# Dealing the query and key projections out beside the HGRN units, and moving twenty adaLN slabs beside the neighbourhood attention tiles

## The reference

```python
h = modulate(rms_norm(x, norm1_g[l]), sh1, sc1)          # latent and context
q, k, v, hq, hf, hb, hi, hg, ga, gh = split(h @ w_in[l])  # 12 blocks of 512 columns
o_na = neighbourhood_attention(rope(q), rope(k), v, ...)  # 8 heads, window + context keys
o_hg = hgrn2_bidirectional(silu(hq), hi, hf, hb)          # 4 heads, scans both ways
x = x + g1 * ((sigmoid(ga) * (o_na @ w_na_o) + sigmoid(gh) * (norm(o_hg) * silu(hg) @ w_hg_o)) @ w_out[l])
h2 = modulate(rms_norm(x, norm2_g[l]), sh2, sc2)
x = x + g2 * grouped_moe(h2)                              # 16 experts, top 2
```

## Time and profile before

| | us |
|---|---|
| median of 3 runs | 2262.05 (2261.82 to 2262.33) |
| the profiled execution | 2260.14 |
| its span, first to last instruction | 2258.3 |
| mean granted TensorE clock | 0.944 |
| HGRN loop, layer 0 / layer 1 (164.8 to 343.9 / 1397.7 to 1531.3) | 179.1 / 133.6 |
| attention tiles, layer 0 / layer 1 (425.6 to 509.0 / 1587.0 to 1639.0) | 83.4 / 52.0 |

### The profile page before, as it was taken

How to read it: one execution, slowest core, us unless ns; L and a number is a source line. 1 busy time by engine, 2 the same in 40 slices (tenths; PEclk the granted TensorE clock), 3 DMA queues, 4 the chain that set the end, 5 groups by cost and what they waited for, 6 DMA issues and landing times.

```text
span 2258.3 us, 21335 instructions
## 1 busy us (share of the span) xinstructions
PE 1986.0 (88%) x7884; PEld 1304.1 (58%) x7884; DVE 1134.5 (50%) x1562; ACT 777.5 (34%) x892; POOL 753.8 (33%) x276
## 2 busy tenths in 40 slices
PE   6998789989999789898999799789899788888886
PEld 2445555444444477777777454546388566666664
DVE  3146652473011566667665433532721576666664
ACT  2222221241000365455555122221410455555553
POOL 0004432100000175556665001423000356666663
PEclk8999999899999899999999799999899899999998
DMA  9330407201204165566554443315124266666661
GB/s 363 127 119 19 149 29 233 111 1 38 75 0 149 38 224 197 211 223 223 210 203 145 150 149 112 118 56 163 37 78 180 98 229 235 223 223 223 220 211 36
DMA packets 160809, 329.02 MB, mean 146 GB/s; under 512 B 21072, under 2 KB 22224, under 8 KB 160720
## 3 DMA queue, kind: packets, MB, share of 16 engines
q1 hardware_dynamic: 143312, 323.66, 39.9%
q10 hardware_dynamic: 17408, 4.20, 1.2%
HBM read 326.79 MB, written 1.05 MB: 145 GB/s over the span
## 4 chain that ended last, share of the span: by engine, by line
PE 58%; DVE 15%; POOL 11%; issue 10%; ACT 5%; DMA 1%; SPq 1%; PEldq 0%; DVEq 0%; POOLq 0%; ACTq 0%
PE bank L374 19%; POOL ring_lo L1220 11%; PE bank L385 5%; PE bank L589 4%; PE bank L577 4%; PE bank L646 3%; ACT w_hi L1087 2%; PE bank L751 2%; PE bank L720 2%; PE bank L444 2%; PE bank L341 2%; DVE ring_lo L1626 2%; DVE pick L1605 2%; DVE pickw L1609 2%; PE bank L549 2%
## 5 line engine op out<-in xcount | busy, mean ns | idle before, releaser
L1220 POOL TENSOR_TENSOR ring_lo<-ring,w_hi 128x2048 fp32r<-128x2048 f32 (+1 forms) x96 | 586.2, 6118 | 894.1 <-ACT w_hi L1087 894.1
L374 PE MATMUL bank<-hT,ring 128*128 128x512 f32 (+1 forms) x1280 | 479.8, 530 | 12.5 <-DVE hT L1307 12.0
L374 PEld LDWEIGHTS bank<-hT,ring 128*128 128x128 f32 x1280 | 246.7, 195 | 226.4 <-issue 198.6
L1087 ACT ACTIVATE w_hi<-ring 128x4096 fp32r<-128x4096 f32 x96 | 347.7, 3621 | 14.3 <-PEq L294 14.3
L1626 DVE TENSOR_TENSOR ring_lo<-ring,w_hi 128x2048 fp32r<-128x2048 f32 (+1 forms) x96 | 236.1, 2460 | 125.0 <-ACT w_hi L1087 124.8
L720 PE MATMUL bank<-ring_lo,picked_hi 128*128 128x512 f32 x512 | 141.6, 421 | 54.5 <-POOL ring_lo L1220 31.9
L1315 DVE SCALAR_TENSOR_TENSOR xT<-bank,mod,xT 128x256 f32<-128x256 f32 x216 | 97.6, 481 | 153.0 <-PE bank L751 77.4
L1177 POOL TENSOR_TENSOR dec<-pf 128x512 f32<-128x512 f32 (+1 forms) x32 | 28.2, 880 | 432.3 <-DVE pb L1352 288.1
L720 PEld LDWEIGHTS bank<-ring_lo,picked_hi 128*128 128x128 f32 x512 | 96.6, 197 | 94.0 <-POOL ring_lo L1220 46.5
L646 PE MATMUL bank<-hrow_hi,pick 128*128 128x512 f32 x192 | 95.2, 496 | 52.4 <-DVE pickw L1609 52.4
L715 PE MATMUL bank<-w_hi,picked_lo 128*128 128x512 f32 x512 | 128.4, 393 | 1.4 <-DVE picked_lo L1617 1.4
(11 more groups left out here) (207 smaller groups left out, 2912.2 us busy)
## 6 DMA issues: line engine op xcount, KB each, us to landing
ring<-in_w_gate SPq DMA_DIRECT2D x32, 2048.0 KB, 8.4
ring<-in_w_up SPq DMA_DIRECT2D x32, 2048.0 KB, 9.0
ring<-in_w_down SPq DMA_DIRECT2D x32, 2048.0 KB, 7.7
ring<-in_w_ada SPq DMA_DIRECT2D x24, 2048.0 KB, 13.8
ring<-in_w_in SPq DMA_DIRECT2D x24, 2048.0 KB, 8.4
ring<-in_w_out SPq DMA_DIRECT2D x4, 2048.0 KB, 10.5
bias_skew<-in_rel_bias_reversed ACTq DMA_DIRECT2D x64, 64.0 KB, 3.8
ring<-in_w_na_o SPq DMA_DIRECT2D x2, 2048.0 KB, 12.3
```

The source lines that it names most:

```text
L374: mm = T.matmul(o[:, lo:TOK], w[:, k, c * P:(c + 1) * P], hT[:, k, lo:TOK], start=(k == 0), stop=(k == KT - 1))
L1087: S.activation(w_hi[m % 2][:], ring[:, s, :], ACT.Copy).then_inc(sem["w_hi_ready"], 1)
L1220: G.tensor_tensor(ring_lo[:, s, a], ring[:, s, a], w_hi[(3 * e + g) % 2][:, a].bitcast(f32), ALU.subtract).then_inc(sem["w_lo_ready"], 1)
```

## The change

1. *Slabs.* The twenty later adaLN slabs leave the projections, the HGRN loop and the value, rope and gate stage. Slabs 4 to 19 are worked beside the attention tiles of layer 0, one at the end of every odd tile (1 to 31), slabs 20 to 23 in layer 1 at the ends of tiles 3, 6, 9 and 12 (`beside_tile`). The rows of slab m are followed by the turn of slab m-1; ScalarE copies in its tile n, VectorE adds in its iteration n + 4.
2. *Projections.* The 64 products of the query and key projections are dealt out over the 38 units, one or two behind each (`project_beside`). They have two PSUM banks (6 and 7) and a semaphore of their own; the loop's other work turns over six banks. ScalarE copies a finished projection two units later in its own order (`keep_beside`).
3. *Ring.* A list `lane` names the slot of each slab; a slab waits for the last one in its slot. The input slabs 3, 4, 5, 6, 0, 1, 2, 7 come first, then the adaLN slabs, then those of the merge. The experts' slabs keep n % 4.

```diff
-        loads = []
+        loads, lane = [], []
+        order = (2, 0, 3, 1)
...
 
         ada_loads = [("ada", l, s) for l in range(DEPTH) for s in range(12)]
...
+        lane += order
         for l in range(DEPTH):
-            a = ada_loads[12 * l + 4:12 * l + 16]
-            loads += [("in", l, 3), a[0], ("in", l, 4), a[1], ("in", l, 5), a[2], ("in", l, 6)]
-            loads += [("in", l, 0)] + a[3:6] + [("in", l, 1)] + a[6:9]
-            loads += [("in", l, 2)] + a[9:11] + [("in", l, 7)] + a[11:12]
+            loads += [("in", l, s) for s in (3, 4, 5, 6, 0, 1, 2, 7)]
+            turn = [0, 1, 2, 3, 0, 1, 2, 3]
+            loads += ada_loads[4:20] if l == 0 else ada_loads[20:24]
+            turn += [0, 1, 2, 3, 0, 1, 2, 3, 0, 1, 2, 3, 0, 1, 3, 1] if l == 0 else [0, 1, 3, 1]
             loads += [("in", l, 8), ("nao", l), ("in", l, 9), ("hgo", l), ("in", l, 10), ("in", l, 11)]
+            turn += [2, 3, 0, 1, 2, 3]
             loads += [("out", l, 0), ("out", l, 1)]
-            assert len(loads) % SLOTS == 0
+            turn += [0, 2]
+            lane += [order[x] for x in turn]
...
             for ph, n in ((2 * l, N_EXPERTS), (2 * l + 1, 3 * N_EXPERTS if l == 0 else N_EXPERTS)):
                 loads += [("moe", ph, e, k) for e in range(n) for k in range(3)]
+            lane += [n % SLOTS for n in range(len(lane), len(loads))]
...
-            return ring[:, slot_of(key) % SLOTS, :]
+            return ring[:, lane[slot_of(key)], :]
...
-            return slot_full[n % SLOTS], 16 * (n // SLOTS + 1)
+            return slot_full[lane[n]], 16 * lane[:n + 1].count(lane[n])
+
+        def last_in(n):
+
+            return max(m for m in range(n) if lane[m] == lane[n])
 
...
+        turns = [0]
+        main_banks = [8]
+        sides = [0]
...
+        def beside_tile(l, n):
+
+            if l == 0:
+                return 4 + n // 2 if n % 2 == 1 and 0 < n < 32 else None
+            return 19 + n // 3 if n in (3, 6, 9, 12) else None
...
-            def open_bank(key, who):
-
-                b = jobs[0] % 8
-                jobs[0] += 1
+            def open_bank(key, who, side=False):
+
+                if side:
+                    b = 6 + sides[0] % 2
+                    sides[0] += 1
+                    ready[key] = (b, sides[0], "side_ready")
+                else:
+                    b = turns[0] % main_banks[0]
+                    turns[0] += 1
+                    jobs[0] += 1
+                    ready[key] = (b, jobs[0], "psum_ready")
...
-                ada = 12 * l + 4
                 for s, who in ((3, "q_ready"), (4, "k_sig"), (5, "k_sig")):
                     pe.wait_ge(*full(("in", l, s)))
                     for c in range(4):
                         project(l, s, c, who, lo if s == 3 else 0)
-                        if c == 0 and s > 3:
-                            ada_turn(ada + s - 4)
-                    ada_rows(ada + s - 3)
                 pe.wait_ge(*full(("in", l, 6)))
                 for t in range(4):
                     project_rows(l, 6, t, "v_ready")
-                    if t == 0:
-                        ada_turn(ada + 2)
...
-                extra = [(s, c) for s in (0, 1) for c in range(4)]
-
-                def between():
-                    if not extra:
-                        return
-                    s, c = extra.pop(0)
-                    if c == 0:
-                        pe.wait_ge(*full(("in", l, s)))
-                    project(l, s, c, "naqk_ready", lo if s == 0 else 0)
-
+                main_banks[0] = 6
+                turns[0] = 0
+
+                def project_beside(first, end):
+
+                    for m in range(first, end):
+                        s, c, k = m // 32, m // 8 % 4, m % 8
+                        w = slot(("in", l, s)).rearrange("p (k n) -> p k n", k=KT)
+                        a = lo if s == 0 else 0
+                        if m % 32 == 0:
+                            pe.wait_ge(*full(("in", l, s)))
+                        if k == 0:
+                            beside[0] = open_bank(("in", l, s, c), "naqk_ready", side=True)
+                        mm = T.matmul(beside[0][:, a:TOK], w[:, k, c * P:(c + 1) * P], hT[:, k, a:TOK],
+                                      start=(k == 0), stop=(k == KT - 1))
+                        if k == KT - 1:
+                            mm.then_inc(sem["side_ready"], 1)
+                        if m % 32 == 31:
+                            slot_spent[slot_of(("in", l, s))] = (sem["side_ready"], sides[0])
+
+                beside = [None]
                 u = 38 * l
                 for hp in range(2):
                     for unit in range(19):
...
                         u += 1
-
-                        n = ada + 3 + 3 * hp + (unit - 5) // 4
-                        if unit in (5, 9, 13) and n < len(ada_loads):
-                            ada_rows(n)
-                        if unit in (7, 11, 15) and n < len(ada_loads):
-                            ada_turn(n)
-                        if unit % 4 == 3:
-                            between()
-                while extra:
-                    between()
+                        v = 19 * hp + unit
+                        project_beside(v * 64 // 38, (v + 1) * 64 // 38)
+                main_banks[0] = 8
 
...
-                if l == 0:
-                    ada_rows(13)
...
                         .then_inc(sem["psum_ready"], 1)
-                if l == 0:
-                    ada_turn(13)
...
                     project(l, 7, c, "hgate_ready", lo)
-                    if l == 0 and c == 0:
-                        ada_turn(14)
-                if l == 0:
-                    ada_rows(15)
                 pe.wait_ge(sem["rope_done"], 8 * (l + 1))
-                if l == 0:
...
+                    m = beside_tile(l, n)
+                    if m is not None:
+                        ada_rows(m)
+                        if m not in (4, 20):
+                            ada_turn(m - 1)
+                ada_turn((19, 23)[l])
...
-                    if n - SLOTS not in slot_spent:
+                    if last_in(n) not in slot_spent:
                         break
-                    sp.wait_ge(*slot_spent[n - SLOTS])
+                    sp.wait_ge(*slot_spent[last_in(n)])
...
-                        n = ada + 3 + 3 * hp + (unit - 6) // 4
-                        if unit in (6, 10, 14) and n < len(ada_loads):
-                            ada_keep(n)
-                        if unit % 4 == 0 and unit and extra:
-                            between()
+                        v = 19 * hp + unit - 2
+                        if v >= 0 and (v + 1) * 64 // 38 // 8 > v * 64 // 38 // 8:
+                            keep_beside()
...
+                    m = beside_tile(l, n)
+                    if m is not None:
+                        ada_keep(m)
...
+                    if m is not None:
+                        ada_mod(m)
                 if stop <= 10 * l + 4:
```

More of the change, by code:

```diff
@@ L209, in build @@
         loads += ada_loads[0:4]
+        lane += order
         for l in range(DEPTH):
-            a = ada_loads[12 * l + 4:12 * l + 16]
-            loads += [("in", l, 3), a[0], ("in", l, 4), a[1], ("in", l, 5), a[2], ("in", l, 6)]
-            loads += [("in", l, 0)] + a[3:6] + [("in", l, 1)] + a[6:9]
-            loads += [("in", l, 2)] + a[9:11] + [("in", l, 7)] + a[11:12]
+            loads += [("in", l, s) for s in (3, 4, 5, 6, 0, 1, 2, 7)]
+            turn = [0, 1, 2, 3, 0, 1, 2, 3]
+            loads += ada_loads[4:20] if l == 0 else ada_loads[20:24]
+            turn += [0, 1, 2, 3, 0, 1, 2, 3, 0, 1, 2, 3, 0, 1, 3, 1] if l == 0 else [0, 1, 3, 1]
             loads += [("in", l, 8), ("nao", l), ("in", l, 9), ("hgo", l), ("in", l, 10), ("in", l, 11)]
+            turn += [2, 3, 0, 1, 2, 3]
             loads += [("out", l, 0), ("out", l, 1)]
-            assert len(loads) % SLOTS == 0
+            turn += [0, 2]
+            lane += [order[x] for x in turn]
+            assert all(lane.count(i) * SLOTS == len(loads) for i in range(SLOTS)), [lane.count(i) for i in range(4)]
             for ph, n in ((2 * l, N_EXPERTS), (2 * l + 1, 3 * N_EXPERTS if l == 0 else N_EXPERTS)):
                 loads += [("moe", ph, e, k) for e in range(n) for k in range(3)]
+            lane += [n % SLOTS for n in range(len(lane), len(loads))]
         def slot(key):
-            return ring[:, slot_of(key) % SLOTS, :]
+            return ring[:, lane[slot_of(key)], :]
         def full(key):
             n = slot_of(key)
-            return slot_full[n % SLOTS], 16 * (n // SLOTS + 1)
+            return slot_full[lane[n]], 16 * lane[:n + 1].count(lane[n])
+        def last_in(n):
+            return max(m for m in range(n) if lane[m] == lane[n])
         ready, reader, last_use, spent = {}, {}, {}, {}
@@ L239, in is_ready @@
         def is_ready(key):
-            return sem["psum_ready"], ready[key][1]
```

(16 more changed lines are left out.)

16 lines of the change are left out of this document (2 added, 14 removed).

## The result

The kernel after takes 2176.36 us (median of 4 runs, 2175.21 to 2179.59), the kernel before beside it 2262.19 us (4 runs, 2261.82 to 2266.35): ratio 0.9619, 95% interval 0.9602 to 0.9636. That is 86 us less; the forecast was 62 less. The profiled execution took 2175.21 us with a span of 2173.4.

What follows compares the result with a forecast made beforehand. TensorE, busy 88% of the span, was taken as the bound, with its idle time and lowered clock to win. Terms -16 -9 -47 -38.5 +39 +9.4 = -62 took 2260.1 to 2198, stated as 2200 us; range 2176 to 2231.

Steps and rivals of the forecast that it cites:

- Slabs out of the projections: Projection stages of both layers, bound by TensorE: three slabs of 2.66 us leave each, 8.0 us gained twice.
- the main case: Whole kernel: everything goes as forecast, 2186 to 2214 us; chance 58%.
- The bound set at the start: TensorE's idle time in the two HGRN loops and layer 0's attention (33, 27, 9 us) is all reordering can win.
- Loops: HGRN loops with projections dealt out and slabs gone: layer 0 from 179.1 to 132 us, layer 1 from 133.6 to 95.
- The step that was wrong: HGRN loop, layer 0: a projection block costs 5.5 of its 6.87 us, because only one finished fac is stored.
- Attention of layer 0: Sixteen slabs added, 42.6 us of TensorE work, 4 us filling idle time: +39, stage 122 us, clock loss unchanged.
- SP's queue: Slab loads during layer 0's attention: asked for eight tiles ahead, all land in time; zero cost.
- second: HGRN loops: the GpSimd-VectorE ring slows when TensorE is dense, +21 and +9 us, 2230 us; chance 13%.
- third: Clock stays up in the attention stage and at cross units: 10 and 3 to 5 us less, 2186; chance 12%.
- fourth: Layer 0's attention: slabs arrive late, one at a time, +8 to +18 us, 2213 us; chance 8%.
- fifth: Slower: clock drops to 1.2 GHz through layer 0's attention stage, +102 us, 2302 us; chance 5%.
- sixth: HGRN loops: dealt products hide nothing, loops 163 and 120 us, +31 and +25, 2256 us; chance 4%.

Runs made afterwards that it cites:

- run 5: Kernel after with projections in blocks of eight again, but ScalarE's copy one exponential later than in the kernel before: 2218.4 us, ratio 0.981.
- run 7: Kernel before with one condition changed, ScalarE's copy one exponential later; nothing dealt out, no slab moved: 2237.47 us, ratio 0.9894.
- run 3: Kernel after with projections in blocks of four products behind every second unit: 2188.82 us, ratio 0.967.
- run 6: Kernel after with ScalarE's copy of a finished projection one exponential earlier: 2179.76 us, ratio 0.9639.
- run 8: Kernel after with slabs at the ends of even attention tiles (layer 1: tiles 2, 6, 8, 12): 2165.51 us, ratio 0.9574.
- run 4: Kernel after with layer 0's sixteen slabs beside tiles 16 to 31, one each, asked for twice as fast: 2175.48 us, ratio 0.9607.

## Why the prediction came out as it did

**Slabs out of the projections: right.** Forecast -8.0 each, measured -7.9 and -8.0. Two rows of a timeline, added up, priced it.

**The whole: right in direction, at the very edge in size.** 2176.36 us lies just inside the stated range (2176 to 2231) and below the band of the main case (2186 to 2214). That it lies inside at all is partly luck: the attention stage of layer 0 came out 5 us longer than forecast, the loops 18 shorter, and 5.5 us lie in experts that the change does not touch. The bound set at the start, that the idle stretches (33, 27 and 9 us) are all that a reordering can win, was wrong: 31 of the 85 us are busy time, most of it clock.

**Loops: right in kind, too small by 18 us.** Forecast -47 and -38.5, measured -54.5 and -49.5. TensorE's work in layer 0 was forecast at 125 and came out at 122.6; the cross units were taken at 4.5 and took 3.6, as the clock stayed up. In layer 1 the work was 79.4 for 84.6. The larger part is the idle time: 7 forecast (its terms add up to 6.2) and 2 measured in layer 0, 10 and 4.5 in layer 1. I had kept 1 us of the wait ahead of each cross unit in layer 0, 3.5 and 0.5 in layer 1, and 2 and 3 for unevenness. In layer 0 no cross unit waits. In layer 1 the first still does, 1.25 and 0.40 us, and the uneven first half costs about 0.7.

**The step that was wrong.** "The projection costs 5.5 of its 6.87, because only one finished fac is in store" takes the one fac for the cause. There are two fac buffers, and with the copy out of the way a block leaves two units in store (runs 5 and 7). It was ScalarE's copy, ahead of an exponential, that kept the second from being filled. Of the 5.5 us the copy is 2.1 (16.8 us over the eight blocks of layer 0, run 7) or 2.6 (20.6, run 5); the rest stays, as a block of 6.9 us outlasts two units in store. I named this wait later in the same part, as "one or two us each, eight times". That price was near: 24 us over the sixteen blocks of both layers of the kernel before, 39 in the blocks of eight. What was missing is that it is part of the 5.5. The forecast's sum adds up TensorE's work unit by unit and did not use the step, so it did not suffer by it; run 3's expectation did use it, and missed by 44 us. For the kernel after I wrote that the copy "costs nothing", and run 6 bears that out within what can be told.

**Values and gate: -9 forecast, -12.8 measured.** The idle time of 2.5 went, and 2 us more by a clock of 1.00 for 0.98.

**Attention of layer 0: +39 forecast, +43.9 measured**, inside the ends. I had 4 us of idle time filled; the stage has 8.8 idle in 127.4, against 9.3 in 83.4 before, so next to nothing was filled. By my own argument nothing could be: both waits, 0.44 and 0.70, fall on the even-to-odd step, which the slabs behind odd tiles miss. And a slab costs 2.83 us here, not 2.66: in the tiles the turn takes 0.98 from start to start (368.54 to 369.52), where rows 4 gave 0.81; sixteen times that is 2.7. Four tiles without a half-speed stretch stand 15.05 apart, not 14.7. The clock's loss, taken as unchanged at 10 us, was 8.9 (0.07 x 127.4), but in five short stretches instead of one long one; that filling the waits would give it back was in no term of the sum, and run 8 shows that it was the larger half.

**Layer 1's attention: +9.4 and +8.4. SP's queue: zero, right** (run 4).

**The experts: zero forecast, -5.5 measured** in layer 0 of the profiled run, at a clock of 0.96 for 0.95. Kernels that differ only elsewhere gave 500.7 to 506.3; why is open.

**Rivals.** The ring did not slow down (second: one fac product of each unit took 1.5 to 1.6 us as before, and units stood 3.3 apart). The forecast said of rows 3 that GpSimd's pieces and VectorE's fac products never run side by side; their records do overlap, from 263.31 to 264.27, and the product took 1.50 us there against 0.69 alone (276.07 in the same trace), so it hardly advanced while GpSimd's piece ran. The clock stayed up at the cross units but not in the attention stage (third, in half). No slab was late (fourth); no stage went to 1.2 GHz throughout (fifth); the dealt products hid what they should (sixth). The oscillating clock of the Trainium skill, "TensorE: Matmul & The Clock Gate", section "A second HAM failure mode: psum-queue depth-cycling", does not show in the loops: both ran at 1.00 with more groups than before. The forecast also spoke of more banks; they are the same eight as before, six in turn and two at the side.

## What to carry to other kernels

Before a long block of TensorE work is cut up, look at what stands behind its result in the queue of the engine that reads it: a copy of 0.6 us one place too early cost 24 us here, and one changed condition gave them back. Filler work belongs exactly where TensorE waits; the same slabs one tile earlier gave 11 us, more of it from the clock than from the waits. And a collision in a stage that no edit touched came and went here by a tenth of a microsecond, so read the untouched stages before an edit is called good or bad.

## What was not expected of the hardware

- A VectorE product of 128x256 takes 0.43 us or 4.80 us by whether it starts 0.16 us before or 0.01 us after a GpSimd subtraction of 4.5 us. In each stage of experts, in the kernel before and in the one after, 15 of 32 such small products (pick and pickw, 128x256 or 128x512) take 4.6 to 5.1 us.
- In a stage that is 93% busy, with fifteen waits of at most 0.7 us, the granted clock fell to 0.50 for 3 to 4 us five times. With three waits left, up to 1.26 us long, the stage of 112.5 us held 1.00, at 299 GB/s of DMA beside it.
- Slabs of 2 MB asked for once per tile landed after 12.6 us, for 8.0 us at half that rate.
